# Four MLPs of a two-block transformer: the first product as seven block products in groups of four tiles, the second product behind each group

## The chip, the cores and the metric

The kernel runs on one core of one Trainium2 chip. The metric is device time in microseconds (us), the median of several executions; lower is better. The chip offers TensorE (matrix products, weight loads beside them), VectorE (DVE), ScalarE (ACT), GpSimd (POOL) and SyncE (SP), each working through its own queue in order, and DMA queues that bring weights from HBM.

## The reference

Two blocks of two layers each, in 32-bit floats. The stream is 512 tokens x 1024 features; the first layer of the first block also carries 256 context tokens through its MLP. Every layer ends in an MLP with squared ReLU, and these four MLPs are what the change is about:

```python
def _sq_relu_mlp(h, w1, w2):          # w1: 1024 x 4096, w2: 4096 x 1024
    a = jnp.maximum(h @ w1, 0)
    return (a * a) @ w2
# block 1, layer l:  x = _layer_norm(ALPHA * x + g2 * mlp(h), ...)   (l = 0: also for the 256 context tokens)
# block 2, layer i:  h_lat = h_lat + mod_l[5] * mlp(_modulate(_rmsnorm(h_lat, ...), ...))
```

The vectors g2, mod_l and their like come from matrix-vector products of a condition with a 1024 x 6144 matrix per layer.

## The kernel before

**Layout and precision.** Activations lie feature-major: 128 features on the partitions, tokens along the free axis (768 in the MLP `l0`, 512 in `l1`, `s0` and `s1`). A weight tile is 128 x 1024 floats, eight 128x128 blocks, 512 KB. Every product is made of three matmuls in a reduced format: both operands are split into a high part, rounded (`act_split`, ACT, L593, for weights), and a low part, the rest (`dve_split`, DVE, L624), and TensorE adds high x high, low x high and high x low. So each weight tile costs one ACT and one DVE instruction on 128x1024 and 24 matmuls per 512 tokens. `whi` has three slots for high parts (`NS`), so ACT can split tile i+2 once TensorE is through with tile i-1. Raw tiles land in four slots (`NR`), from the MLP `s0` on in nine (`XR` = 5 more; one more high slot, `XS`).

**Queues.** `Tiles` lists all weight tiles in the order in which TensorE uses them; `act_tiles` and `dve_tiles` bring the splits of the tiles ahead into ACT's and DVE's queues. All queues are written out at build time and strictly in that order; the engines meet at semaphores (`wait_ge`). A PSUM bank is claimed by TensorE for a result and freed by whoever read it (`claim`, `freed`).

**MLPs `l0`, `l1`** (`mlp`, `pe_mlp`, `act_mlp`, `dve_mlp`). Four rounds q; each makes eight fc1 tiles (ACT: ReLU out of PSUM L1253, DVE: square L1277, ACT: high part L1255, DVE: low part L1280), and then eight fc2 tiles over these eight, each added to the stream by DVE (`dve_add_gated`, L925: one instruction per 512 or 256 tokens). 

**MLPs `s0`, `s1`** (`second_mlp`, `pe_quads`, `act_quads`, `dve_quads`). The first eight fc1 tiles as above. The other 24 come in groups of four (Q = 2 to 7), each as seven block products after Strassen and Winograd: inputs and weights are cut in halves of features and tokens, four sums or differences of the input (`operand`, L2630 and L2636, once per MLP) and of the weights (`dve_block_sum`, L603, per group) are formed, and seven products replace eight (`product`, L2511: 24 matmuls of 256 tokens each). DVE adds the products out of PSUM into four cells of SBUF (`second_sums` L2658, L2663; `third_sums` L2671, L2675; `corner_sum` L2683), one for each quarter ("corner") of the result; ACT squares each (`corner_high`: ReLU L2582, high part L2584, square L2585), and DVE takes the low part (`corner_low`, L2688). After two groups come eight fc2 tiles. The last corner depends on the last product.

**Modulation jobs** (`modulation`, only in `l0`: 132 items, 128 of them tiles; and `s0`: 49, 48 tiles). They compute the condition vectors of later layers beside the MLP: for each tile ACT issues a 512 KB load (L692) into one of `NM` = 3 slots and DVE multiplies it with the condition and sums (L732). The items are dealt out evenly over steps 2 to 61 of the MLP's 64; a step stands at the same place of all queues:

```python
elif i in number:                     # ACT, in act_step, for the n-th tile of the step
    ACTQ.wait_ge(*at("dve_job", (name, n)))
    act_send(n + NM)
...                                   # DVE, in dve_step
    DVEQ.wait_ge(*at(f"job_in{n % NM}", (name, n)))
    dve.scalar_tensor_tensor(x, x, 1.0, sil[:, :], ...)
```

In `l0` a step follows each fc1 and each fc2 tile. In `s0` a step follows each of the first 16 tiles, and from then on two steps follow each fc2 tile and none stands among the block products (`second_steps`, L2485).

Of the kernel before, what the change touches and what calls it, by code (L numbers as in the profile page):

```python
# [13 lines left out]
P = 128  # L14
# [138 lines left out]
class Tiles:  # L153
# [46 lines left out]
    def place_blocks(self):  # L200

        first = min(self.start)
        G = self.alloc.index(self.keys[first])
        self.grown_at, self.slot, self.slot_after = first, {}, {}
        for a, key in enumerate(self.alloc):
            if G <= a < G + XR:
                self.slot[key], self.slot_after[key] = NR + a - G, ("mixout", 0)
# [4 lines left out]
        self.high, self.high_after = {}, {}  # L212
        for i, key in enumerate(self.keys):
            if first <= i < first + XS:
                self.high[key], self.high_after[key] = NS + i - first, ("mixout", 0)
                continue
            r = i - NS - (XS if i >= first else 0)
            before = self.keys[r] if r >= 0 else None
            self.high[key], self.high_after[key] = (i if before is None else self.high[before]), before

    def highs_upto(self, i):
        return min(i + NS + (XS if i >= self.grown_at - NS else 0) - self.hold[self.keys[i]], len(self.keys))

    def lows_upto(self, i):
        return min(i + NS - self.hold[self.keys[i]], len(self.keys))
# [49 lines left out]
XR, XS = 5, 1  # L275


class Parts:


    def __init__(self, parts):
        self.parts = parts

    def __getitem__(self, place):
        p, k, n = place
        return self.parts[k // 4][p, k % 4, n]


def quad_order(t, name):
    t.tile((name + "fc1", 0))  # L290
    t.tile((name + "fc1", 1), 1)
    for m in range(NK):
        if m > 1:
            t.tile((name + "fc1", m))
        t.mark((name, "evict", 0, m))
    for q in range(4):
        if q:
            t.quad(name + "fc1", 2 * q)
            t.quad(name + "fc1", 2 * q + 1)
        for m in range(NK):  # L300
            t.tile((name + "fc2", 8 * q + m))
    t.mark((name, "end"))


def mlp_order(t, name):
    t.tile((name + "fc1", 0))
    t.tile((name + "fc1", 1), 1)
    for q in range(4):
        for m in range(NK):
# [3 lines left out]
        for m in range(NK):  # L313
            t.tile((name + "fc2", 8 * q + m))
    t.mark((name, "end"))
# [64 lines left out]
def tile_order():  # L380
# [27 lines left out]
    quad_order(t, "s0")  # L408
# [3 lines left out]
    quad_order(t, "s1")  # L412
# [4 lines left out]
def program(nc, din, out, known):  # L417
# [77 lines left out]
    def high_of(key):  # L495
        n = seq.high[key]
        return whi[:, n, :] if n < NS else more["hi"][:, n - NS, :]
# [89 lines left out]
    def act_split(a):  # L587
# [3 lines left out]
        if seq.high_after[key]:  # L591
            ACTQ.wait_ge(*at("pe_tile", seq.index[seq.high_after[key]]))
# [34 lines left out]
    def act_tiles(upto):  # L627
        for key in seq.until("act", upto):
# [10 lines left out]
            for a in range(seq.come.get("hi", 0), seq.highs_upto(i)):  # L639
# [212 lines left out]
    def pe_dense(keys, Hh, Hl, hi_at, lo_at, ranges, bank=None, order=range(NK)):  # L852
# [8 lines left out]
        for k in order:  # L861
            PEQ.wait_ge(*hi_at(k))
            ws = slice(P * k, P * k + P)
            for key, acc, i, hi, lo in both:
                for w in (hi, lo):
                    for o, m, _ in ranges:
                        pe.matmul(acc.ap[:, o:o + m], w[:, ws], Hh[:, k, o:o + m], start=k == order[0] and w is hi, stop=False)  # L867
            PEQ.wait_ge(*lo_at(k))
            for key, acc, i, hi, lo in both:
                for o, m, _ in ranges:  # L870
                    ins = pe.matmul(acc.ap[:, o:o + m], hi[:, ws], Hl[:, k, o:o + m], start=False, stop=k == order[-1])  # L871
                if k == order[-1]:
# [280 lines left out]
    def ln_h(N, Hh, Hl):  # L1153
# [3 lines left out]
        act_ln_h(N, Hh)  # L1157
# [39 lines left out]
    def mlp(L, name, htag, ranges, Hh, Hl, after, centered, columns=None, beside=None, weights=None, jobs=None):  # L1197
# [4 lines left out]
        keys = [fc2(name, 3, m) for m in range(NK)]  # L1202
        with ExitStack() as s:
            Ah, Al = sb(s, [P, NK, n], F32R), sb(s, [P, NK, n], F32R)
            r1 = [sb(s, [P, n]) for _ in range(2)]
            r2 = [sb(s, [P, n]) for _ in range(2)]
            N = Norm(after, ranges, [sb(s, [P, n]) for _ in range(4)], centered, updated_at(keys, after, centered), weights)
            pe_by, act_by, dve_by = beside(s) if beside else [lambda t: None] * 3
            pe_step = act_step = dve_step = pool_all = None
            if jobs:  # L1210
                pe_step, act_step, dve_step, pool_all = modulation(name, sb(s, [P, 1024]), jobs, 2, 62)
            begin_stage("pool")
            pe_mlp(name, htag, ranges, Hh, Hl, Ah, Al, N, keys, pe_by, pe_step)
            act_mlp(L, name, n, Ah, r1, r2, N, act_by, act_step)
            if jobs:
                pool_all()
            dve_mlp(L, name, htag, ranges, n, Ah, Al, r1, r2, N, columns, dve_by, dve_step)
        return N

    def fc1(name, q, m):  # L1220
        return name + "fc1", 8 * q + m

    def fc2(name, q, m):
        return name + "fc2", 8 * q + m

    def pe_mlp(name, htag, ranges, Hh, Hl, Ah, Al, N, keys, beside, step):
        hh, hl = h_parts(htag)
        pe_dense([fc1(name, 0, 0), fc1(name, 0, 1)], Hh, Hl, hh, hl, ranges)
        for q in range(4):
            for m in range(NK):  # L1230
                if 8 * q + m > 1:
                    pe_dense([fc1(name, q, m)], Hh, Hl, hh, hl, ranges)
# [2752 lines left out]
```

## Time and profile before

| | |
|---|---|
| median of 3 runs | 3005.75 us (3005.33 to 3008.53) |
| the profiled execution | 3008.25 us, its span 3006.9 us |
| TensorE busy | 2856.6 us of the span, 16898 matmuls |
| DVE, ACT, POOL busy | 1736.5, 1146.9, 339.4 us |
| TensorE clock granted, mean | 0.981 of 2.4 GHz |
| MLP `l0`, from its first matmul to its last tile | 515.2 to 1065 us |
| MLP `l1` | 1452.7 to 1831 us |
| MLP `s0` | 2233.7 to 2590 us |
| MLP `s1` | 2640.6 to 2992 us |

A time of an instruction is from its start to its end as the profiler has it. Matmuls are pipelined, so the time that one costs in a stream is the length of a stretch over their number and not the duration shown. The same holds in small for DVE and ACT: of two instructions that follow each other, the second starts some 0.09 us before the first is shown to end.

### The profile page before, as it was taken

What the parts mean: (1) busy time and instruction counts of PE and PEld (TensorE: products, weight loads), DVE (VectorE), ACT (ScalarE), POOL (GpSimd) and SP (SyncE); (2) the same over time, 40 slices, a digit from 0 to 9 for tenths busy, and PEclk for the clock granted to TensorE, in tenths of its full rate; (3) what the DMA queues carried; (4) which work ended last, traced back from release to release, by engine and by line L of the source; (5) the groups of instructions that cost most, each with busy time, mean ns of one, the idle gap of its engine ahead of it and who ended that gap; (6) DMA issues with size and microseconds to landing.
All of it is one profiled execution on the core that took longest, in us unless ns stands there. A gap on an engine that the chain in (4) does not pass through costs nothing.

```text
span 3006.9 us, 41839 instructions
## 1 busy us (share of the span) xinstructions
PE 2856.6 (95%) x16898; PEld 2283.9 (76%) x16898; DVE 1736.5 (58%) x2638; ACT 1146.9 (38%) x1895; POOL 339.4 (11%) x371
## 2 busy tenths in 40 slices
PE   7999999999999989999999998998889999899998
PEld 6766667888888866767677776776667999679986
DVE  3656544656565656654554445646736888556664
ACT  4245443412222242554422334312643444444442
POOL 2022210300000030321201002000510000110000
PEclk9999999999999999999999999999999999999999
DMA  7222001556555511001232332312034555323321
GB/s 281 77 98 80 9 21 43 177 195 210 172 207 185 186 55 49 9 15 42 76 113 91 98 99 64 102 56 70 1 116 137 175 176 176 126 70 99 94 90 63
DMA packets 88487, 315.87 MB, mean 105 GB/s; under 512 B 9991, under 2 KB 12295, under 8 KB 88040
## 3 DMA queue, kind: packets, MB, share of 16 engines
q1 hardware_dynamic: 59040, 213.94, 21.8%
q10 hardware_dynamic: 29256, 99.26, 9.6%
q8 instruction: 135, 2.21, 0.3%
q14 instruction: 56, 0.46, 0.0%
HBM read 311.06 MB, written 2.10 MB: 104 GB/s over the span
## 4 chain that ended last, share of the span: by engine, by line
PE 55%; DVE 4%; ACT 3%; issue 1%; POOL 1%; ACTq 0%; DVEq 0%; POOLq 0%
PE bank L867 22%; PE bank L871 11%; PE bank L2511 8%; PE bank L1370 2%; PE bank L3484 2%; PE bank L1431 1%; PE bank L1387 1%; PE bank L1862 1%; PE bank L2257 1%; PE bank L1981 1%; PE bank L3256 1%; PE bank L977 1%; ACT t L593 0%; PE bank L3562 0%; PE bank L1379 0%
## 5 line engine op out<-in xcount | busy, mean ns | idle before, releaser
L867 PE MATMUL bank<-t 128*128 128x512 f32 x5600 | 1493.7, 369 | 28.5 <-ACT t L1173 7.5
L867 PEld LDWEIGHTS bank<-t 128*128 128x128 f32 x5600 | 958.7, 189 | 244.2 <-issue 51.8
L871 PE MATMUL bank<-t 128*128 128x512 f32 x2800 | 908.9, 368 | 5.9 <-POOL t L1182 5.7
L593 ACT ACTIVATE t<-t 128x1024 fp32r<-128x1024 f32 x386 | 404.9, 1054 | 708.6 <-PE bank L871 450.5
L624 DVE TENSOR_TENSOR t<-t 128x1024 fp32r<-128x1024 f32 x386 | 474.6, 1234 | 242.7 <-ACT t L593 240.9
L871 PEld LDWEIGHTS bank<-t 128*128 128x128 f32 x2800 | 478.3, 189 | 109.3 <-POOL t L1182 13.0
L925 DVE SCALAR_TENSOR_TENSOR t<-bank,t 128x512 f32<-128x512 f32 x192 | 129.6, 693 | 342.5 <-PE bank L871 327.4
L2511 PEld LDWEIGHTS bank<-t 128*128 128x128 f32 x2016 | 240.1, 189 | 0.5
L2511 PE MATMUL bank<-t 128*128 128x256 f32 x2016 | 240.2, 281 | 0.0
L732 DVE SCALAR_TENSOR_TENSOR t<-t 128x1024 f32<-128x1024 f32 x176 | 209.5, 1223 | 6.5 <-DMA t<-in_mod 6.2
L1571 POOL TENSOR_SCALAR t<-t 128x768 f32<-128x768 f32 (+3 forms) x160 | 126.2, 792 | 522.2 <-DVE t L1539 522.1
L1370 PE MATMUL bank<-t 64*128 64x384 f32 (+2 forms) x768 | 136.1, 472 | 16.5 <-ACT t L1469 5.2
L1514 DVE TENSOR_REDUCE t<-bank 128x1 f32<-128x768 f32 (+1 forms) x120 | 96.6, 845 | 88.2 <-PE bank L1379 68.0
L1459 ACT ACTIVATE t<-bank 128x384 f32<-128x384 f32 (+1 forms) x160 | 73.7, 460 | 171.9 <-PE bank L1387 171.5
L993 ACT ACTIVATE t<-t 128x512 f32<-128x512 f32 (+1 forms) x64 | 43.8, 685 | 248.1 <-DVE t L925 176.1
L1387 PEld LDWEIGHTS bank<-t 128*128 128x128 f32 x784 | 85.8, 141 | 59.2 <-issue 29.7
L1387 PE MATMUL bank<-t 128*128 128x128 f32 x784 | 121.2, 282 | 10.0 <-DVE t L1525 7.0
L1469 ACT ACTIVATE t<-bank,t 128x768 f32<-128x768 f32 (+3 forms) x160 | 124.3, 781 | 14.0 <-DVE t L1514 8.0
L1277 DVE TENSOR_TENSOR t<-t 128x768 f32<-128x768 f32 (+1 forms) x64 | 54.1, 845 | 94.1 <-ACT t L1253 94.1
L1431 PE MATMUL bank<-t 128*64 128x128 f32 x1568 | 105.1, 281 | 2.0 <-DVE t L1545 2.0
L1370 PEld LDWEIGHTS bank<-t 64*128 64x128 f32 x768 | 67.0, 188 | 52.3 <-issue 22.6
L1431 PEld LDWEIGHTS bank<-t 128*64 128x64 f32 x1568 | 85.7, 139 | 15.6 <-issue 13.2
(340 smaller groups left out, 2637.1 us busy)
## 6 DMA issues: line engine op xcount, KB each, us to landing
t<-in_mod ACTq DMA_DIRECT2D x176, 512.0 KB, 4.1
t<-in_l0fc SPq DMA_DIRECT2D x64, 512.0 KB, 3.9
t<-in_l1fc SPq DMA_DIRECT2D x64, 512.0 KB, 3.5
t<-in_s0fc SPq DMA_DIRECT2D x64, 512.0 KB, 3.6
t<-in_s1fc SPq DMA_DIRECT2D x64, 512.0 KB, 3.5
t<-in_mod SPq DMA_DIRECT2D x48, 512.0 KB, 4.4
t<-in_mixin SPq DMA_DIRECT2D x24, 512.0 KB, 3.4
t<-in_l0in SPq DMA_DIRECT2D x12, 512.0 KB, 3.6
```

Source lines behind the costliest of these rows:

```text
L593: act.activation(high_of(key), landed_of(key), ACT.Copy).then_inc(*up("act_whi", a))
L624: dve.tensor_tensor(low_of(key), landed_of(key), high_of(key).bitcast(F32), ALU.subtract).then_inc(*up("dve_wlo", a))
L732: dve.scalar_tensor_tensor(x, x, 1.0, sil[:, :], ALU.mult, ALU.mult, accum_out=modt[L][:, j, s:s + 1]).then_inc(*up("dve_job", (name, n)))
L867: pe.matmul(acc.ap[:, o:o + m], w[:, ws], Hh[:, k, o:o + m], start=k == order[0] and w is hi, stop=False)
L871: ins = pe.matmul(acc.ap[:, o:o + m], hi[:, ws], Hl[:, k, o:o + m], start=False, stop=k == order[-1])
L925: ins = dve.scalar_tensor_tensor(x[:, o:o + n], acc.ap[:, o:o + n], mcol(L, part, k, s), x[:, o:o + n], ALU.mult, ALU.add)
L1370: ins = pe.matmul(places[side][:, 512 * r + o:512 * r + o + m], g["q"][side](c), g["k"][side][:, k0:k0 + m], start=r not in begun, stop=last)
L1387: ins = pe.transpose(turns[r].ap[:, P * b:P * b + P], p[:, P * i:P * i + P], mat("ident"))
L1431: ins = pe.matmul(b6.ap[64 * side:64 * side + 64, 0:P], g["v"][side](kb), PT[(2 * u + side) % 3][:, r, b, :], start=i == 0, stop=i == len( ...
L1469: act.activation(keys_of(p, g), scores_of(ps[side], g), ACT.Exp, bias=row[:, 7:8], accum_out=row[:, 3:4]).then_inc(*ps[side].freed((tag, u ...
L1571: pool.tensor_scalar(x, x, stat(u, side)[:, 7:8], 1.0, ALU.mult, ALU.mult).then_inc(*up("pool_prob", (tag, u, side)))
L2511: ins = pe.matmul(bank.ap[:, 256 * pair:256 * pair + 256], w[:, ws], x, start=pair == 0 and k == 0 and w is hi and x is h, stop=pair == 1 ...
```

## The change

All four MLPs run one new routine `mlp`. Its group Q = 0 is four plain fc1 tiles; the groups Q = 1 to 7 are seven block products each. Behind each group stand four fc2 tiles of a new cut: each holds two output tiles (of eight) over the group's four fc1 tiles, so that every output is added to the stream eight times instead of four. In `l0` a product has 24 matmuls of 384 tokens and spans two PSUM banks (a pair called ps); there are three pairs, and the outputs use ps1 and ps0 in turn. The four operands are now formed before the four evictions of Q = 0, and their splits stand beside the first fc2 tiles. There are eight raw weight slots from `l0` on, and three high slots throughout. The input's plain copy (`F`) has eight buffers. The steps of the modulation jobs stand behind products 1, 3 and 5 and behind the fc2 tiles, two of them behind the second. A barrier between normalization and MLP in `l0` and `l1` falls away.

```diff
 BLOCKS = (0, 4, 5, 3)
 NR, NS, NM, NE = 4, 3, 3, 14
-XR, XS = 5, 1
+XR = 4
...
 def mlp_order(t, name):
     t.tile((name + "fc1", 0))
     t.tile((name + "fc1", 1), 1)
-    for q in range(4):
-        for m in range(NK):
-            if 8 * q + m > 1:
-                t.tile((name + "fc1", 8 * q + m))
-            t.mark((name, "evict", q, m))
-        for m in range(NK):
-            t.tile((name + "fc2", 8 * q + m))
+    for m in range(2, 4):
+        t.tile((name + "fc1", m))
+    for Q in range(8):
+        if Q:
+            t.quad(name + "fc1", Q)
+        for j in range(4):
+            t.tile((name + "fc2", 4 * Q + j))
     t.mark((name, "end"))
...
+    BLOCK_SUMS = {4: (1, 4, 5, ALU.add), 3: (4, 0, 4, ALU.subtract), 2: (2, 1, 0, ALU.subtract), 1: (6, 3, 2, ALU.subtract)}
...
     def dve_tiles(upto):
...
-                for a in range(seq.come.get("lo", 0), seq.lows_upto(i)):
+                dve_quad_sums(i, 2)
+                for a in range(seq.come.get("lo", 0), min(i + NS - seq.hold[key], len(seq.keys))):
                     dve_split(a)
-                dve_quad_sums(i)
+                dve_quad_sums(i, 4, 3, 1)
...
+    PRODUCT_BANKS = {NT: (0, 1, 2, 3, 0, 2, 3), T: (2, 0, 1, 2, 1, 2, 0)}
+    OUT_BANKS = {NT: (1, 0, 2, 3), T: (1, 0)}
...
+    def steps_beside(Q, p):
+
+        return (8 * Q + (p - 1) // 2,) if p in (1, 3, 5) else ()
+
+    def steps_behind(Q, j):
+
+        return ([8 * Q + 3], [8 * Q + 4, 8 * Q + 5], [8 * Q + 6], [8 * Q + 7])[j] if Q else (4 + j,)
...
+        def outputs(Q, j):
...
+            if j == 0:
+                for s in range(2):
+                    PEQ.wait_ge(*banks[s].claim(out_of(name, Q, 2 * j + s)))
+                for ks in ((1, 3), (0, 2)) if Q else ((0, 1), (2, 3)):
+                    for s in range(2):
+                        for k in ks:
+                            high(s, k, k == ks[0] and ks[0] < 2 and ks[0] == (1 if Q else 0))
+                    for s in range(2):
+                        for k in ks:
+                            low(s, k, k == ks[1] and ks[1] == (2 if Q else 3))
+                return
+            for s in range(2):
+                PEQ.wait_ge(*banks[s].claim(out_of(name, Q, 2 * j + s)))
+                for k in range(4):
+                    high(s, k, k == 0)
+                    low(s, k, k == 3)
...
+        for Q in range(8):
...
+            else:
+                for p in range(7):
+                    if p == 3:
+                        second_sums(Q)
+                    if p == 4:
+                        corner_sum(Q, 0)
+                    if p == 5:
+                        third_sums(Q)
+                    if p == 6:
+                        corner_sum(Q, 2)
+                    dve_tiles(quad(name, Q, p))
+                    if p in (5, 6):
+                        corner_low(Q, {5: 0, 6: 3}[p])
+                    if step:
+                        for s in steps_beside(Q, p):
+                            step(s)
+            for j in range(4):
+                if j == 0 and Q:
+                    corner_sum(Q, 1)
+                    corner_low(Q, 2)
+                    corner_low(Q, 1)
+                dve_tiles(fc2(name, Q, j))
...
+                if step:
+                    for s in steps_behind(Q, j):
+                        step(s)
+                for m in (2 * j, 2 * j + 1):
+                    update(Q, m)
```

`act_mlp` has the same shape: behind product p it runs `act_tiles`, at p = 4, 5 and 6 `corner_high` of corners 0, 3 and 2, then the steps; before the first fc2 tile `corner_high` of corner 1. `update` does what `dve_add_gated` did. The corners 0, 1, 2 and 3 rest on products 3, 6, 5 and 4.

## Rows read from the trace of the kernel before

**Rows 1.** The page's first part: busy us (share) x instructions; and the granted clock.

```profile
PE 2856.6 (95%) x16898; PEld 2283.9 (76%) x16898; DVE 1736.5 (58%) x2638; ACT 1146.9 (38%) x1895; POOL 339.4 (11%) x371
...
PEclk9999999999999999999999999999999999999999
```

**Rows 2.** Windows in `l0` and `s0`: length, busy us (x) by engine, clock, DMA.

```profile
721.80:789.00 67.20, 67.20 (x389) 58.66 (x388) 42.53 (x63) 11.19 (x13) 0.99 (x5) 1.00 0.62 210
2334.04:2374.05 40.01, 40.01 (x337) 40.01 (x337) 33.56 (x38) 27.00 (x37) 0.00 (x0) 1.00 0.46 149
2374.05:2418.63 44.58, 44.58 (x194) 36.04 (x194) 35.63 (x48) 10.49 (x12) 0.00 (x0) 1.00 0.62 196
```

**Rows 3.** Groups of PE by form: busy us, mean ns, idle before.

```profile
L2511 PE MATMUL bank<-t 128*128 128x256 f32 x2016 | 240.2, 281 | 0.0
...
L3484 PE MATMUL bank<-t 128*128 128x512 f32 x192 | 46.4, 398 | 1.9 <-DVE t L1746 1.7 <-DVE t L925 0.3
```

**Rows 4.** Line L2257 over the whole span: duration min/median/max of its two forms.

```profile
L2257 PE MATMUL bank<-t x240: 277/337/446, 164.6 to 1363.6; 128*128 128x384 f32 x72, 128*128 128x256 f32 x48
```

**Rows 5.** Groups of DVE in `l0`, 560 to 1000 us.

```profile
L732 DVE SCALAR_TENSOR_TENSOR t<-t 128x1024 f32<-128x1024 f32 x111 | 131.0, 1220 | 0.1
L624 DVE TENSOR_TENSOR t<-t 128x1024 fp32r<-128x1024 f32 x52 | 63.7, 1225 | 47.4 <-ACT t L593 46.4
L1280 DVE TENSOR_TENSOR t<-t 128x768 fp32r<-128x768 f32 x28 | 26.8, 958 | 25.5 <-ACT t L1255 25.5
...
L925 DVE SCALAR_TENSOR_TENSOR t<-bank,t 128x512 f32<-128x512 f32 x24 | 18.0, 750 | 65.4 <-PE bank L871 63.7 <-ACT t L722 1.6
L925 DVE SCALAR_TENSOR_TENSOR t<-bank,t 128x256 f32<-128x256 f32 x24 | 11.4, 475 | 0.0
```

**Rows 6.** Groups of ACT in `l0`, 560 to 1000 us.

```profile
L593 ACT ACTIVATE t<-t 128x1024 fp32r<-128x1024 f32 x53 | 56.2, 1061 | 264.4 <-PE bank L871 143.1 <-DVE t L732 121.3
L1255 ACT ACTIVATE t<-t 128x768 fp32r<-128x768 f32 x28 | 23.7, 846 | 31.5 <-DVE t L1277 31.5
```

**Rows 7.** Timeline of ACT in `l0`: start, us, instruction, idle before.

```profile
720.43 0.34 ACTq L692 DMA_DIRECT2D t<-in_mod  x1
720.81 1.06 ACT L593 ACTIVATE t<-t 128x1024 fp32r<-128x1024 f32 x1 [3.70 <-DVE t L732]
```

**Rows 8.** Timeline of DVE in `l0`, the same place.

```profile
719.17 1.22 DVE L732 SCALAR_TENSOR_TENSOR t<-t 128x1024 f32<-128x1024 f32 x1
...
721.98 1.23 DVE L624 TENSOR_TENSOR t<-t 128x1024 fp32r<-128x1024 f32 x1 [1.57 <-ACT t L593]
```

**Rows 9.** DMA issues of the page: KB each, median us from issue to landing.

```profile
t<-in_mod ACTq DMA_DIRECT2D x176, 512.0 KB, 4.1
```

**Rows 10.** Timeline of DVE in `s0`, from the fifth product's end on (group 3).

```profile
2368.46 0.69 DVE L2671 TENSOR_TENSOR t<-bank,t 128x512 f32<-128x512 f32 x1 [1.13 <-PE bank L2511]
...
2371.52 0.68 DVE L2683 TENSOR_TENSOR t<-bank,t 128x512 f32<-128x512 f32 x1
2372.13 1.21 DVE L624 TENSOR_TENSOR t<-t 128x1024 fp32r<-128x1024 f32 x1
...
2374.09 0.69 DVE L2683 TENSOR_TENSOR t<-bank,t 128x512 f32<-128x512 f32 x1
```

**Rows 11.** Timeline of ACT in `s0`, the same stretch.

```profile
2371.63 1.04 ACT L593 ACTIVATE t<-t 128x1024 fp32r<-128x1024 f32 x1
2372.58 0.62 ACT L2582 ACTIVATE t<-t 128x512 f32<-128x512 f32 x1
2373.22 0.63 ACT L2584 ACTIVATE t<-t 128x512 fp32r<-128x512 f32 x1
```

**Rows 12.** Timeline of PE: the stalls in the opening of `s0` and `s1`.

```profile
2256.49 0.70 PE L867 MATMUL bank<-t 128*128 128x512 f32 x2 [2.45 <-DVE t L624]
...
2292.07 0.73 PE L867 MATMUL bank<-t 128*128 128x512 f32 x2 [2.43 <-ACT t L2570]
...
2662.35 1.19 PE L867 MATMUL bank<-t 128*128 128x512 f32 x2 [2.58 <-DVE t L624]
```

**Rows 13.** Window of the opening of `s0`, columns as in Rows 2.

```profile
2290.00:2334.00 44.00, 41.93 (x173) 33.40 (x174) 30.41 (x37) 9.95 (x10) 0.00 (x0) 0.96 0.46 149
```

**Rows 14.** Groups of DVE in `l1`: the sine argument of the filter beside the MLP.

```profile
L2893 DVE SCALAR_TENSOR_TENSOR t<-t 64x512 f32<-64x512 f32 x6 | 4.1, 682 | 0.2
```

More of the change, by code:

```diff
@@ L495, in high_of @@
     def high_of(key):
-        n = seq.high[key]
-        return whi[:, n, :] if n < NS else more["hi"][:, n - NS, :]
+        return whi[:, seq.index[key] % NS, :]
     def landed_at(key):
@@ L638, in act_tiles @@
             i = seq.index[key]
-            for a in range(seq.come.get("hi", 0), seq.highs_upto(i)):
+            for a in range(seq.come.get("hi", 0), min(i + NS - seq.hold[key], len(seq.keys))):
                 act_split(a)
@@ L850, in program, with pe_dense @@
     acc_of = {}
-    def pe_dense(keys, Hh, Hl, hi_at, lo_at, ranges, bank=None, order=range(NK)):
+    def pe_dense(keys, Hh, Hl, hi_at, lo_at, ranges, bank=None):
         both = []
@@ L860, in pe_dense @@
             PEQ.wait_ge(*acc.claim(key))
-        for k in order:
+        for k in range(NK):
             PEQ.wait_ge(*hi_at(k))
@@ L866, in pe_dense @@
                     for o, m, _ in ranges:
-                        pe.matmul(acc.ap[:, o:o + m], w[:, ws], Hh[:, k, o:o + m], start=k == order[0] and w is hi, stop=False)
+                        pe.matmul(acc.ap[:, o:o + m], w[:, ws], Hh[:, k, o:o + m], start=k == 0 and w is hi, stop=False)
             PEQ.wait_ge(*lo_at(k))
@@ L1215, in mlp @@
             if jobs:
                 pool_all()
[L1217 to L1226, printed above, removed]
-        hh, hl = h_parts(htag)
[L1228 to L1232, printed above, removed]
-                if step:
-                    step(16 * q + m)
-            for m in range(NK):
-                pe_dense([fc2(name, q, m)], Ah, Al, lambda k: at("act_ahi", (name, q, k)),
-                         lambda k: at("dve_alo", (name, q, k)), ranges)
-                if q == 3:
-                    pe_norm_step(N, m, acc_of[keys[0]].after(keys[0]))
-                beside(8 * q + m)
-                if step:
-                    step(16 * q + 8 + m)
-        pe_tiles((name, "end"))
@@ L2741, in dve_quads, with second_mlp @@
-        dve_tiles((name, "end"))
+            dve.tensor_tensor(work[:, k % 4, :], XT[k][:, 0:NT], ps[2].ap[:, 0:NT], ALU.mult).then_inc(*done)
+        for k in range(NK):
+            POOLQ.wait_ge(*at("act_hhi", (N.tag, k)))
+            POOLQ.wait_ge(*at("act_h", (N.tag, k)))
+            pool.tensor_tensor(Hl[:, k, :], F[:, k, :], Hh[:, k, :].bitcast(F32),
+                               ALU.subtract).then_inc(*up("pool_hlo", (N.tag, k)))
+    def second_mlp(L, N, after, columns, jobs=None):
+        return mlp(L, f"s{L - 2}", N, LAT, after, False, lambda Hh, Hl, F, cells: second_h(N, L, Hh, Hl, F, cells),
+                   columns, jobs=jobs)
@@ L3552, in products @@
             PEQ.wait_ge(*ps[g % 2].claim(("pool v", g)))
-            for bank in fours[2 * (g % 2):2 * (g % 2) + 2]:
-                PEQ.wait_ge(*bank.after(bank.order[-1]))
             for kk in range(2):
```

753 lines of the change are left out of this document (331 added, 422 removed).

## The prediction

> **What bounds the kernel now.** I read the page first: TensorE is busy 95% of the span at a full clock [rows 1]. Then windows inside the MLPs, each cut from tile to tile: there TensorE never idles. Eight fc1 tiles of `l0` fill 67.2 of 67.2 us, two groups of block products in `s0` 40.0, eight fc2 tiles 44.6 [rows 2]. DVE stands at 63% in `l0` and at 80 to 84% in `s0`, ACT at 17 to 67%. Last the idle time of these two: DVE waits for ACT's splits, ACT for TensorE and for DVE's jobs [rows 5, 6]. So TensorE's stream sets the end, and DVE is the engine that comes next.
>
> **What the stream gains.** Per matmul: 44.58/192 = 0.232 us at 512 tokens, 40.01/336 = 0.119 at 256, and 67.2/192 = 0.350 for the pair 512 + 256 of `l0` [rows 2]. The trace has no long stream of 384. Durations shown are 281, 337 and 398 ns at 256, 384 and 512 [rows 3, 4], evenly spaced, so 384 lies midway between 0.119 and 0.232: 0.176. A plain group of four tiles has 96 matmuls per token range: 33.6 us in `l0`, 22.3 elsewhere. Seven products have 168: 29.6 and 19.95. Gain 4.03 us per group in `l0`, 2.33 elsewhere. Seven groups are new in `l0` (-28.2), seven in `l1` (-16.3), one each in `s0` and `s1` (-2.4 each): -49.3 us in all. fc2 has the same matmuls in another order, and the weight loads stay 64 tiles per MLP.
>
> For 384 columns the Trainium skill, "TensorE: Matmul & The Clock Gate", Back-to-back issue gap, gives N/2.4 + 2.5 ns. That is an estimate of 162.5 ns, and 28.2 would become 44. The rows are above that formula at both neighbouring widths (119 against 109, 232 against 216).
>
> **What DVE and ACT get.** A DVE instruction that follows another costs its duration less 0.09: 1.135 for a split or block sum, 0.87 for 768 tokens, 1.145 for a job, 1.06 for an update of 768 in two pieces [rows 5]. ACT: 0.95 a split, 0.75 for 768 [rows 6], 0.34 to issue a load [rows 7]. For one group of `l0` DVE does 11 splits (12.5), 4 block sums (4.5), 7 sums out of PSUM and 4 low parts (9.6), 8 updates (8.5, twice as many as now per group) and 17.6 jobs (20.2): 55 us in a TensorE group of 29.6 + 33.6 = 63.2. That is 87%, and behind the products 33 of 33.6. The queues are strictly in order, so what counts is what stands ahead of the instruction that TensorE waits for.
>
> **A group of `l0`, step by step.** I laid the three queues side by side in their new order; every instruction starts when the one ahead is through and what it waits for is there, 0.04 to 0.13 us after it. Group 3 stands for the rest (0 = start of product 0, products end every 4.22). Product 2 ends at 12.7. DVE: two sums, a split and the two jobs of the step at p = 3, until 18.1. ACT's split of the next tile stands behind its two sends, and each waits for its job. So it is now too: the split starts only after a job ends, and DVE's follows 1.57 us late [rows 7, 8]. Corner 0 until 19.0, split 20.8, third sums 21.2 to 23.0, split and low part to 25.1, three jobs of p = 5 to 28.5, corner 2 to 29.4, split (after ACT's) 31.2, low part 32.1. Only then comes corner 1, whose sum frees ps0, and ps0 is claimed by the first outputs: it ends 33.1, while TensorE was through at 29.6. **Stall 3.6.** With DVE on time it would still be 1.2, for the sum itself.
> From there (0 = first output, corner 1 freed) the first output is made at 7.7 and DVE, after two low parts, split, block sum and two jobs, updates it at 8.1 to 9.2; TensorE wants the bank back at 8.4. **Stall 0.8** (0.7 with no jobs). Then update, split, block sum, and two steps with four or five jobs. There are three load slots: the fourth job's load is sent after the first job and lands 4.1 us later [rows 9], so DVE waits 2.2 us and updates output 2 at 19.2 to 20.3; TensorE wants it at 17.6. **Stall 2.7 to 3.9.** The other outputs come in time. The same walk over all eight groups gives for Q = 1 to 7, 20.5 at the claim, 7.9 at output 2 and 25.7 at output 4; 3.7 more at Q = 7, where output 3 waits for the shift of the norm in the same bank; and 9.7 in Q = 0, where four operands of 1.7 us, their low parts and the updates crowd DVE. Together 67 us. `l0`: -28.2 + 67.4 = **+39**.
>
> **`s0`.** Four single banks take away the bank waits. But jobs now stand among the products, and TensorE's first output matmul needs corner 2. In the trace its sum runs at 2371.52, ACT's split at 2371.63, ReLU at 2372.58 and the high part 2373.22 to 2373.85; TensorE starts on fc2 at 2373.95 [rows 10, 11]: 0.1 us in hand. One job at p = 5 puts DVE's 1.145 and ACT's send (0.34) and wait ahead of that: high part at 2375.4, stall 1.4. A job at p = 3 too makes it 3.1, at all three 4.1. With 49 items over 60 steps the walk gives 17.6 for seven groups; 0.5 for low parts; 2.6 in Q = 0. Gone are the two stalls of the opening (4.9) [rows 12] and a half-rate stretch behind the second (44 us at a clock of 0.96 [rows 13], so 44 x 0.04 = 1.8 of lost cycles). `s0`: -2.4 + 20.7 - 6.7 = **+11.6**.
> **`l1`** has no jobs; each later group is just in time [rows 10, 11]. In Q = 0 DVE has splits, block sums, operand low parts, updates and the filter's sine arguments (two times 4.9, three instructions of 0.68 in each [rows 14]): 29 us in 22.3, which I price at 7.7 of stalls before product 2 of Q = 1; 1.1 of present ones go. -16.3 + 6.6 = **-9.7**.
> **`s1`** has neither: -2.4, and its stall of 2.6 [rows 12] with some 1.4 of half rate goes, 1.2 comes in Q = 0: **-5.2**.
> **Clock.** Behind two of the three stalls of 2.4 to 2.6 us the clock fell to half [rows 12, 13]; the cost was some 1.7 us each. `l0` and `s0` will have some 17 of that size. Part of it lies under DVE's lateness, so I take +5 (bounds 0 and 29).
> Weight slots, eight instead of four between the MLPs: no stall of TensorE outside them is put down to a load, so 0 (bounds -3, +1).
> Sum: 39.2 + 11.6 - 9.7 - 5.2 + 5 = 40.9 on a span of 3006.9. The profiled execution took 3008.25 against a median of 3005.75, 2.5 us that I do not carry over: 3005.75 + 40.9 = 3046.6, rounded to **3046**.
>
> The price of the queue order rests on strict order: DVE was idle for 1.57 us behind a job that ACT had to answer [rows 8]. The Trainium skill says the same of ACT and DVE, strict FIFO, in "TensorE: Matmul & The Clock Gate", Architectural detail; by it no later instruction slips past a job, and by the trace none does.
>
> **Rivals.**
> *The stalls of `l0` and `s0` are mostly absorbed* (other side). DVE's load is below 100% in every phase; if its instructions reach TensorE in time but for the structural 1.2 + 0.7 per group of `l0` and 3.7 at its end, `l0` has 19 us (-9), `s0` 3 (-6), with -9.7 and -5.2: -30, 2976; with nothing stalling at all -60, 2946. It decides from where the stalls of `l0` and `s0` together fall below 47 of 88 us. For it: DVE has some slack now [rows 5]. Against: its slack is not at the place of the chain. 0.20.
> *Half of the stalls*: the third load slot or the last corner is in time more often than I walk it. Within 6 us of before: 0.04; between 3012 and 3030, 0.10.
> *My forecast*, 3030 to 3065: 0.52.
> *The stalls let the clock fall each time*, 17 x 1.7 = 29 instead of 5, or job loads take 4.5 us (+5): 3065 to 3085. 0.09.
> *384 columns stream at 0.1625 or less.* As a mechanism: at 256 the weight load fills all of its queue, 40.01 of 40.01 us, in the longer ones it does not [rows 2], so the overhead of 384 may be smaller than midway. 1176 x 0.0135 = 16 us less stream in `l0`, of which DVE's lateness at the claim takes half: 3038. That rule of the skill's page is the reason to count it. 0.05.
>
> **The numbers.** Slower by over 0.2% (6 us, about what a measurement of this kernel can tell): 0.10 + 0.52 + 0.09 + 0.05 = 0.76. Same 0.04, faster 0.20. The range must leave out no more than 0.2: below 2980 I see 0.13 (of the absorbed case those near nothing stalling), above 3075 0.05, so 2980 to 3075. The forecast's own range, from its bounds (clock 0 to 15, `l1` opening 2 to 9, load time 3.3 to 4.5 giving -4 to +5): 3030 to 3065.
>
> **What the profile after would show.** TensorE idle in `l0` by some 67 us, ended by DVE's update and PSUM-sum lines, at the first, third and fifth output of each group; matmuls of 384 in products of 4.22 us; DVE waiting for `in_mod` loads some 2 us per group; in `s0` idle before each group's first output, ended by ACT's square; `l1` and `s1` shorter by 10 and 5 us, group time 42.2. I am wrong if a group of `l0` takes under 67 us from product 0 to product 0, if 384 columns cost more than 0.19 or less than 0.165, or if the stalls lie at weight splits instead of banks.

## The result, and the profile after

The changed kernel takes **3087.4 us** (median of 4 runs, 3081.4 to 3087.9) against 3006.3 for the kernel before on the same chip: ratio 1.026, 95% interval 1.025 to 1.028. Forecast were 3046, range 2980 to 3075. The sign and the stalls of TensorE came as forecast; the clock that they cost did not. The change is +81 us where +41 was forecast, and the time lies above the range.

The page of the changed kernel, the lines that answer to [rows 1, 9]:

```profile
PE 2847.5 (92%) x17378; PEld 2328.5 (75%) x17378; DVE 2031.5 (66%) x2974; ACT 1254.3 (41%) x2031; POOL 346.3 (11%) x371
...
PEclk9999999999999989999999999999999999999999
...
t<-in_mod ACTq DMA_DIRECT2D x176, 512.0 KB, 4.5
```

TensorE is busy for 9 us less in a span that is 80 us longer. Busy time alone would hide half of the loss: a matmul at half rate counts as busy. The windows of the four MLPs without their norms show both. Before (`l0`, `l1`, `s0`, `s1`), columns as in [rows 2]:

```profile
512.00:1066.00 554.00, 550.60 (x3154) 475.28 (x3156) 346.43 (x488) 149.88 (x176) 32.68 (x26) 0.99 0.54 182
1462.00:1829.00 367.00, 366.24 (x1561) 285.18 (x1560) 169.84 (x215) 122.83 (x165) 31.89 (x19) 1.00 0.31 99
2249.00:2590.00 341.00, 336.12 (x1932) 291.12 (x1931) 260.21 (x322) 145.91 (x188) 1.69 (x3) 0.99 0.52 173
2654.00:2992.00 338.00, 335.42 (x1931) 291.35 (x1930) 203.27 (x224) 141.75 (x183) 0.00 (x0) 0.99 0.27 86
```

After (in `l0` from the end of the opening on):

```profile
558.00:1134.00 576.00, 513.86 (x2788) 465.08 (x2788) 430.14 (x585) 170.96 (x193) 2.61 (x10) 0.95 0.51 169
1527.00:1892.00 365.00, 360.26 (x2102) 305.67 (x2100) 279.49 (x333) 172.40 (x232) 41.07 (x22) 0.99 0.32 100
2303.00:2674.00 371.00, 349.74 (x2051) 304.32 (x2049) 296.24 (x368) 158.97 (x206) 7.92 (x9) 0.99 0.49 158
2729.00:3073.00 344.00, 343.17 (x2043) 300.03 (x2043) 240.62 (x269) 156.71 (x203) 7.32 (x6) 1.00 0.28 86
```

`l0` is the place: 62 us idle in 576, and the clock at 0.95, where 1.00 is 2.4 GHz and the half-rate stretches run at 1.2. Who ended the idle time of TensorE (total, times, longest), first in `l0`, then in `s0`:

```profile
PE bank L1296 <- DVE t L1508: 36.5, 19, 5.2
PE bank L1296 <- DVE t L1462: 22.8, 7, 4.0
PE bank L1296 <- ACT t L1372: 7.4, 1, 7.4
```

```profile
PE bank L1296 <- DVE t L582: 19.1, 7, 4.2
```

L1508 is the update of the residual, L1462 a sum out of PSUM (here that of corner 1, which frees `ps0`), L1372 ReLU of a plain tile. L1296 are the matmuls of an fc2 output on the high parts of the activations, L1302 those on the low parts. In group 2 of `l0` one sees the claim, output 2 and output 4:

```profile
699.71 4.24 PE L1274 MATMUL bank<-t 128*128 128x384 f32 x23
707.15 4.60 PE L1296 MATMUL bank<-t 128*128 128x512 f32 x16 [3.21 <-DVE t L1462]
...
718.03 0.94 PE L1296 MATMUL bank<-t 128*128 128x512 f32 x4 [0.63 <-DVE t L1508]
...
725.11 0.51 PE L1302 MATMUL bank<-t 128*128 128x512 f32 x2
...
730.69 1.62 PE L1296 MATMUL bank<-t 128*128 128x512 f32 x4 [4.01 <-DVE t L1508]
732.11 0.84 PE L1302 MATMUL bank<-t 128*128 128x512 f32 x2
```

Behind the last stall two matmuls of L1302 take 0.84 us, before it 0.51. What DVE did until then, five jobs of two steps and their loads:

```profile
721.12 1.21 DVE L691 SCALAR_TENSOR_TENSOR t<-t 128x1024 f32<-128x1024 f32 x1
...
726.05 1.23 DVE L691 SCALAR_TENSOR_TENSOR t<-t 128x1024 f32<-128x1024 f32 x1 [1.42 <-DMA t<-in_mod]
...
728.26 1.23 DVE L691 SCALAR_TENSOR_TENSOR t<-t 128x1024 f32<-128x1024 f32 x1 [0.97 <-DMA t<-in_mod]
729.41 0.08 DVE L691 DVE_READ_ACCUMULATOR t<-t 128x1 f32 x1
729.41 2.19 DVE L1508 SCALAR_TENSOR_TENSOR t<-bank,t 128x512 f32<-128x512 f32 x4
```

And the clock around it, three windows (length, PE busy ..., clock):

```profile
657.04:660.45 3.41, 3.41 (x13) 2.93 (x12) 3.31 (x5) 0.00 (x0) 0.00 (x0) 0.50 0.06 25
728.72:735.55 6.83, 4.86 (x15) 4.21 (x16) 6.73 (x11) 1.06 (x1) 0.00 (x0) 0.50 0.48 153
783.33:790.15 6.82, 5.64 (x17) 4.84 (x18) 5.10 (x6) 3.48 (x5) 0.00 (x0) 0.50 0.07 29
```

In `s0` the walk's place, one group: a job at 2370.02, then the sum for corner 2, ACT's send, split, ReLU, high part, and TensorE.

```profile
2370.02 1.22 DVE L691 SCALAR_TENSOR_TENSOR t<-t 128x1024 f32<-128x1024 f32 x1
...
2371.16 0.68 DVE L1462 TENSOR_TENSOR t<-bank,t 128x512 f32<-128x512 f32 x1
```

```profile
2371.27 0.33 ACTq L651 DMA_DIRECT2D t<-in_mod  x1
2371.71 1.06 ACT L550 ACTIVATE t<-t 128x1024 fp32r<-128x1024 f32 x1 [1.76 <-DVE t L691]
2372.67 0.61 ACT L1389 ACTIVATE t<-t 128x512 f32<-128x512 f32 x1
2373.32 0.63 ACT L1391 ACTIVATE t<-t 128x512 fp32r<-128x512 f32 x1
```

```profile
2374.09 1.62 PE L1296 MATMUL bank<-t 128*128 128x512 f32 x3 [4.15 <-DVE t L582]
```

The trace puts this wait down to a weight split of DVE (L582), which ended at the same moment; the high part (L1391) ended at 2373.95, 0.14 before TensorE. The offsets are the same two in all seven groups, so this trace alone does not decide between them; both stand behind the job. In the sixth run, where the sum for this corner is what is late, the same wait is put down to the high part. It is the chain of [rows 10, 11], with a send and a wait for a job in it.

**Where the 80 us are.** I summed, over successive matmuls, the time from start to start less the spacing of that width (0.119, 0.176, 0.232): over 0.35 us it is a stall, inside a half-rate stretch it is clock. A stall costs 0.16 us more than its idle time, as the matmul ahead is shown until its pipelined end. The lengths are from one norm to the next. The rows add up to the 79.6 us between the two spans.

| us | forecast | measured | of it stalls | of it clock |
|---|---|---|---|---|
| `l0` | +39 | +71.7 | 0.9 to 72.6 | 1.3 to 23.7 |
| `l1` | -9.7 | -8.6 | 1.1 to 4.2 | 0 to 1.8 |
| `s0` mixer | 0 | +5.2 | - | not separated |
| `s0` | +11.6 | +16.6 | 5.2 to 22.7 | 1.6 to 4.7 |
| pool, rest | 0 | -1.3 | | |
| `s1` | -5.2 | -4.0 | 2.7 to 0.9 | 1.4 to 0 |
| clock | +5 | in the rows above | | |

### The profile page after: what moved, and what is told of

It reads as the page before. It is cut to its first block, busy times and chain, and to the rows that moved or that the text cites. A ratio compares the mean times of both kernels' runs of the same rounds, so it can differ in the third digit from the quotient of the medians.

```text
span 3086.5 us, 43456 instructions
## 1 busy us (share of the span) xinstructions
PE 2847.5 (92%) x17378; PEld 2328.5 (75%) x17378; DVE 2031.5 (66%) x2974; ACT 1254.3 (41%) x2031; POOL 346.3 (11%) x371
## 4 chain that ended last, share of the span: by engine, by line
PE 37%; DVE 6%; ACT 4%; issue 2%; POOL 1%; ACTq 0%; DVEq 0%; POOLq 0%
PE bank L1296 11%; PE bank L1274 10%; PE bank L1302 6%; PE bank L826 2%; ACT t L550 2%; DVE t L582 1%; PE bank L3436 1%; PE bank L830 1%; PE bank L2113 1%; ACT t L2681 1%; DVE t L691 1%; PE bank L1621 1%; PE bank L3213 1%; PE bank L936 1%; PE bank L3512 0%
## 5 line engine op out<-in xcount | busy, mean ns | idle before, releaser
L550 ACT ACTIVATE t<-t 128x1024 fp32r<-128x1024 f32 x434 | 456.1, 1054 | 853.1 <-PE bank L1302 352.0
L1296 PE MATMUL bank<-t 128*128 128x512 f32 (+1 forms) x2560 | 700.1, 384 | 88.7 <-DVE t L1508 36.5
L582 DVE TENSOR_TENSOR t<-t 128x1024 fp32r<-128x1024 f32 x434 | 538.3, 1244 | 334.7 <-ACT t L550 330.3
L1274 PE MATMUL bank<-t 128*128 128x256 f32 (+1 forms) x4704 | 632.9, 295 | 3.5 <-issue 2.5
L1274 PEld LDWEIGHTS bank<-t 128*128 128x128 f32 x4704 | 630.0, 188 | 6.8 <-issue 5.0
L1296 PEld LDWEIGHTS bank<-t 128*128 128x128 f32 x2560 | 458.3, 195 | 203.3 <-issue 99.2
L826 PE MATMUL bank<-t 128*128 128x512 f32 (+1 forms) x1568 | 414.1, 374 | 21.9 <-ACT t L1132 7.7
L1302 PE MATMUL bank<-t 128*128 128x512 f32 (+1 forms) x1280 | 408.5, 376 | 0.0
L826 PEld LDWEIGHTS bank<-t 128*128 128x128 f32 x1568 | 270.9, 194 | 88.8 <-issue 37.7
L1508 DVE SCALAR_TENSOR_TENSOR t<-bank,t 128x512 f32<-128x512 f32 x320 | 210.8, 692 | 88.8 <-PE bank L1302 88.1
L1302 PEld LDWEIGHTS bank<-t 128*128 128x128 f32 x1280 | 225.8, 192 | 48.6 <-DVE t L1489 3.4
L830 PE MATMUL bank<-t 128*128 128x512 f32 (+1 forms) x784 | 246.3, 371 | 6.7 <-POOL t L1141 6.6
L1462 DVE TENSOR_TENSOR t<-bank,t 128x512 f32<-128x512 f32 (+1 forms) x196 | 148.0, 755 | 30.2 <-PE bank L1274 25.4
L830 PEld LDWEIGHTS bank<-t 128*128 128x128 f32 x784 | 134.0, 192 | 37.6 <-POOL t L1141 11.7
L560 DVE TENSOR_TENSOR t<-t 128x1024 f32<-128x1024 f32 x112 | 140.7, 1256 | 0.0
```

Of the source, the lines that this page charges most:

```text
L550: act.activation(high_of(key), landed_of(key), ACT.Copy).then_inc(*up("act_whi", a))
L560: dve.tensor_tensor(landed_of(k[p]), landed_of(k[a]), landed_of(k[b]), op).then_inc(*up("dve_sum", k[p]))
L582: dve.tensor_tensor(low_of(key), landed_of(key), high_of(key).bitcast(F32), ALU.subtract).then_inc(*up("dve_wlo", a))
L1274: ins = pe.matmul(dst, w[:, ws], x, start=(pair == 0 or n > NT) and k == 0 and w is hi and x is high, stop=pair == 1 and k == 3 and x is l ...
L1296: pe.matmul(banks[s].ap[:, o:o + m], w[:, ws], Ah[:, k, o:o + m], start=first and w is hi, stop=False)
L1302: ins = pe.matmul(banks[s].ap[:, o:o + m], hi[:, ws], Al[:, k, o:o + m], start=False, stop=last)
```

## The experiments

Theory A: the stalls come from the order of the queues (jobs ahead of an update or a corner) and from two output banks that come back after one output; the half-rate time follows the long stalls. Against it stand: the clock belongs to the new stream (B), and DVE has simply too much to do, so the waits move (C). Each run is compared with runs of the kernel before on the same chip, 3007 to 3009 us. Runs 5 to 10 ran on another chip than the changed kernel and runs 1 to 4, so differences of a few us between the two sets say nothing. The edits are shown shortened, those of runs 2, 3 and 5 partly in words. What a run says of stalls and clock is summed as in the table, from its profiled execution.

**1. Three output banks in `l0`.**

```
-    OUT_BANKS = {NT: (1, 0, 2, 3), T: (1, 0)}
+    OUT_BANKS = {NT: (1, 0, 2, 3), T: (1, 2, 0, 1, 2, 0, 1, 0)}
+    LAST_BANKS = (2, 1, 0, 1, 0, 1, 0, 1)      # T, Q == 7
```

> The changed kernel, but fc2 of l0 goes round three output banks instead of two (ps1, ps2, ps0, ps1, ps2, ps0, ps1, ps0; in the last group ps2, ps1, ps0, ps1, ...). Nothing else moves. Theory A (stalls come from the order of the queues and the reuse of two banks; the half-rate clock follows the long stalls): by the same walk the stalls of TensorE in l0 fall from 71 to about 41 us (none at the claim of ps0 in groups 1 to 7, 1.1 to 2.2 before the second pair of cells' high parts, 0.8 to 1.9 at the sixth output instead of 2.7 to 4 at the fifth, 3.7 and 6.9 left in the last group), and with the stalls over 2.6 us gone from the middle the matmuls at half rate cost some 7 us instead of 24: 3087 - 30 - 17 = 3040. Theory B (the half-rate time belongs to the new stream itself, not to its stalls): stalls fall as in A, the 24 us stay: 3057. Theory C (DVE's load is the bound, so the stalls only go elsewhere): 3075 or more.

3041.5 us, ratio 1.0115 [1.010, 1.013]. Stalls of `l0` 72.6 to 40.3, clock 23.7 to 8.3. No claim waits for the corner any more; ACT's high part of it does:

```profile
PE bank L1298 <- DVE t L1510: 20.4, 10, 4.4
PE bank L1298 <- ACT t L1393: 11.7, 7, 2.3
```

**2. The steps of `l0` elsewhere**, banks as they were.

```
-  steps at products 1, 3, 5; fc2 tiles 0, 1, 1, 2, 3
+  steps at products 0, 2, 4; fc2 tiles 0, 1, 2, 3, 3
```

> The changed kernel, but the eight steps of the modulation jobs in a group of l0 stand behind products 0, 2 and 4, behind the first three fc2 tiles one each, and two behind the fourth (now: products 1, 3 and 5, fc2 tiles one, two, one, one). Banks as in the changed kernel. Theory A: by the walk the stalls of l0 fall from 71 to about 37 us (1.2 to 1.6 at the claim, 0.7 to 2.0 at output 2, none at output 4, 3.7 in the last group; the 3.8 and 4.0 of the first group stay), and the half-rate cost from 24 to about 7: 3087 - 34 - 17 = 3036. Theory B: 3053. Theory C (DVE's load): over 3075, stalls at other places.

3040.9 us, 1.0112 [1.010, 1.013]. Stalls 42.3, clock 7.9. The claims fell from 22.8 to 9.9 us in sum; output 4 waits only in groups 0 and 7:

```profile
PE bank L1298 <- DVE t L1510: 18.9, 12, 4.5
PE bank L1298 <- DVE t L1464: 9.9, 7, 2.0
PE bank L1298 <- ACT t L1374: 7.3, 1, 7.3
```

**3. The steps of `s0` behind fc2.**

```
-  steps at products 1, 3, 5; fc2 tiles 0, 1, 1, 2, 3
+  steps at product 2; fc2 tiles 0, 0, 1, 1, 2, 2, 3
```

> The changed kernel, but in s0 seven of the eight steps of a group stand behind the fc2 tiles (one behind product 2, two behind each of the first, second and third tile, one behind the fourth); l0 as it is. Theory A: the stalls in front of the first output of the seven groups fall from 20 to about 2 us, their half-rate cost from 4.7 to about 1: 3087 - 18 - 3 = 3066. Theory B: 3069. Theory C (the jobs' 1.145 us each come back as stalls at the outputs, whose four banks are then in use): 3080 or more.

3061.7 us, 1.0178 [1.016, 1.019], 4 us below theory A's 3066. `s0` is 358.8 us long instead of 382.7 (before the change 366.2), with 1.4 us of stalls. The 7.4 us below before fit the 2.4 of the products and the 4.9 of the two opening stalls that are gone [rows 12]. So all but 1.4 us of the stalls of `s0` were the jobs in the chain of corner 2.

**4. All three edits.**

> The three edits together: three output banks in l0, the steps of l0 at products 0, 2, 4 and behind fc2, those of s0 behind fc2. Theory A: stalls of l0 about 17 us (6 to 8 in the first group, 5 in the last), half-rate cost there about 5, s0 as in the third run: 3087 - 54 - 19 - 21 = 2993, faster than before the change by 0.4%. Theory B: 3012 to 3016, slower than before. Theory C: over 3050.

2995.2 us, 0.9962 [0.995, 0.997]: faster than before the change. Stalls of `l0` 23.0, clock 7.5. DVE is busy for 462 of 560 us there, 83%, more than the 75% of the changed kernel with its 72.6 us of stalls: against theory C, its load is not the bound.

**5. The products of `l0` undone**: plain fc1 tiles in groups of four; all else of the change stays.

```
-            t.quad(name + "fc1", Q)
+            if name == "l0": four plain tiles 4 * Q + m, evicted like those of group 0
+            (a step behind each fc1 and each fc2 tile; no operands, no corners)
```

> The changed kernel with one part undone: in l0 the seven later groups of fc1 are four plain tiles each again (24 x 768 tokens, 33.6 us per group instead of 29.6), with their eviction as in the kernel before; fc2 behind every four tiles, eight slots, and s0, l1 and s1 stay as changed. A step of jobs behind every tile. Theory A (the products' block sums, PSUM sums and corners are what makes DVE late in l0): stalls of l0 fall from 72 to under 8 us, half-rate cost from 24 to about 2, the stream grows by 28: 3087 - 65 - 22 + 28 = 3028 if 7 are left, and 3012 if l0 is what it was before (562.6 us). I expect 3012 to 3018. Theory B (fc2 by four tiles, with twice as many updates and its banks coming back at 8.4 us, makes the stalls by itself): 3040 or more. The four MLPs other than l0 then leave +6 to +9 against the kernel before.

3083.4 us, 1.0254 [1.024, 1.027]: my expectation fell, theory B's 3040 or more came. Without a single product `l0` is 628.7 us long, with them 634.4. Of its stalls, 44.8 us in all, nine wait for an update, seven of these 3.9 to 5.0 us long at output 2, and the clock costs 20.3 us as well:

```profile
PE bank L1303 <- DVE t L1529: 37.8, 9, 5.0
```

```profile
637.94 1.23 DVE L585 TENSOR_TENSOR t<-t 128x1024 fp32r<-128x1024 f32 x1 [1.57 <-ACT t L553]
639.09 1.22 DVE L694 SCALAR_TENSOR_TENSOR t<-t 128x1024 f32<-128x1024 f32 x1
...
641.38 2.19 DVE L1529 SCALAR_TENSOR_TENSOR t<-bank,t 128x512 f32<-128x512 f32 x4
```

```profile
642.66 0.77 PE L1303 MATMUL bank<-t 128*128 128x512 f32 x1 [5.03 <-DVE t L1529]
```

DVE's load is 351 us in the 576 of the window here, 61%. It is the order: three jobs stand behind the last fc1 tile, then the split that ACT's job send held up by 1.57 us, then two jobs, and then only the update that frees the bank. Before the change an output took 8.4 us and the bank was wanted 8.4 us later; by fours it is wanted after 4.2.

**6. Delays of known length in `s1`**, in the fourth run's kernel.

```
+            if name == "s1" and c == 2:        # ahead of the sum for corner 2
+                for _ in range(Q):
+                    dve.tensor_tensor(tabs[:, 3, :], tabs[:, 0, :], tabs[:, 1, :], ALU.add)
```

> The fourth run's kernel (all three edits) with a delay put in s1: ahead of the sum for corner 2 in group Q, DVE does Q extra additions of 128 x 512, one after the other, Q = 1 to 7. They are work left over, used by nobody. TensorE's first output waits for that corner, with some 0.1 us in hand, so its idle time should be about 0.7 Q: 0.6, 1.3, 2.0, 2.7, 3.4, 4.1, 4.8 us, sum 19. Theory A (the length of the idle time decides what the clock does): no half rate behind the first two or three, a half-rate stretch of 3.4 us behind the fourth and fifth, 6.8 us around the last two, in all some 9 us lost to half rate: 2995 + 19 + 9 = 3023. Theory B (each stall costs the same 1.7 us whatever its length): 7 stretches, 12 us, 3026, with stretches behind the short ones too. Theory C (it is the stream of 768 tokens in l0 that lets the clock fall, not idle time): none in s1, 3014.

3016.7 us in its single run. The seven idle times, group 1 to 7 (three are shown, 2.53, 3.26 and 3.99 lie between), and the clock behind those of groups 3 to 7:

```profile
2698.88 0.47 PE L1300 MATMUL bank<-t 128*128 128x512 f32 x1 [0.36 <-ACT t L1395]
...
2786.83 0.48 PE L1300 MATMUL bank<-t 128*128 128x512 f32 x1 [1.80 <-ACT t L1395]
...
2974.34 0.77 PE L1300 MATMUL bank<-t 128*128 128x512 f32 x1 [4.71 <-ACT t L1395]
```

```profile
2787.00:2831.00 44.00, 42.35 (x264) 37.88 (x263) 32.07 (x38) 17.83 (x23) 0.00 (x0) 1.00 0.32 96
2831.87:2877.00 45.13, 44.05 (x264) 39.14 (x264) 31.84 (x37) 17.56 (x22) 0.00 (x0) 0.96 0.31 94
2879.19:2924.00 44.81, 42.52 (x264) 38.00 (x264) 32.80 (x39) 17.55 (x22) 0.00 (x0) 1.00 0.31 95
2925.70:2970.00 44.30, 43.93 (x264) 39.11 (x264) 31.15 (x36) 17.56 (x22) 0.00 (x0) 0.96 0.19 60
2974.34:3000.00 25.66, 25.66 (x97) 18.89 (x98) 9.68 (x13) 7.94 (x13) 0.00 (x0) 0.89 0.00 1
```

Idle times of 0.4, 1.1 and 1.8 us have no half rate behind them, 2.53 has a stretch of 3.4 us, 3.26 none, 3.99 one of 3.4, 4.71 one of 6.8; 5.8 us are lost. So idle time makes the clock fall in `s1` too, whose products have 256 columns (against C), the cost grows with the length (against this run's B), and in the middle it is not decided by the length alone. The stalls came to 19.6 us, `s1` grew by 24.4 against the fourth run: a delay in this chain goes through in full.

**7. Narrow jobs**: a job's instruction reads 64 of 1024 columns.

```
-  dve.scalar_tensor_tensor(x, x, 1.0, sil[:, :], ...)
+  dve.scalar_tensor_tensor(x[:, 0:64], x[:, 0:64], 1.0, sil[:, 0:64], ...)
```

> The changed kernel, but a job's instruction on DVE reads 64 of its 1024 columns, so the modulation vectors made in l0 and s0 are sums over 64 columns instead of 1024; the loads, their three slots, the waits and the order stay. Theory A (it is the jobs' 1.145 us on DVE that stand ahead of what TensorE waits for): by the walk stalls of l0 fall from 71 to about 33 us (1.2 at each claim, 0.7 at output 2, 0.7 to 1.1 at output 4), those of s0 from 23 to 6, half-rate cost from 29 to about 9: 3087 - 38 - 17 - 20 = 3012. Theory B (it is the jobs' loads, three slots and 4.1 to 4.5 us each, so the stalls at output 4 stay): 25 us more, 3035 or over.

3010.8 us, 1.0011 [1.000, 1.002], for a kernel whose modulation vectors are sums over 64 columns, so it computes something else. Loads, slots and waits are unchanged, and 77 us are gone: it is the 1.145 us on DVE. Left in `l0` are the claims (9.4 us, seven), the first group (6.3) and 15.2 at updates.

**8. The fourth run, jobs of `l0` from step 4 on** (`modulation(..., 4, 62)`).

> The fourth run's kernel with the jobs of l0 spread over steps 4 to 62 instead of 2 to 62, so none of them and no copy of the condition stands between the first group's four plain tiles. By the walk the stalls of the first group fall from some 8 to 1 to 3 us and 1.1 us each come at two products later: 2995 - 3 to - 6 = 2989 to 2992. Theory C (the first group's stalls are those of DVE's operands and their low parts, not of the jobs): 2995, no change.

2992.1 us, 0.9951 [0.994, 0.997]. The stalls of the first group fell from 10.6 to 3.8 us; against the fourth run's 2995.2 the difference is no larger than the spread of either, so the size is inconclusive.

**9. Plain groups in `l0` with three output banks.**

> The fifth run's kernel (plain tiles in all groups of l0) with three output banks instead of two in groups 0 to 6. The fifth run had one stall of 3.9 to 5.0 us in each group, at output 2, for the update of output 0. Theory D (the stalls come from the bank's early return together with the jobs that stand ahead of the update; the products themselves are not needed for it): the third output takes a bank that is free, the update is wanted 4.2 us later, the seven stalls fall from 32 to under 5 us in sum (the last group's 3.9 stays twice, its banks are two), half-rate cost from 20 to about 6: 3083 - 27 - 14 = 3042. Theory E (DVE has too much to do in a group, so the wait moves to outputs 4 and 6): 3070 or more.

3040.6 us, 1.0105 [1.009, 1.012]. Stalls of `l0` 44.8 to 17.1, clock 20.3 to 5.7. In groups 1 to 6 at most one idle time of 0.2 to 0.8 us is left, and the last group's two of 3.9, whose banks are two:

```profile
638.47 0.49 PE L1305 MATMUL bank<-t 128*128 128x512 f32 x1 [0.75 <-DVE t L1531]
...
1046.18 0.76 PE L1305 MATMUL bank<-t 128*128 128x512 f32 x1 [3.90 <-DVE t L1531]
```

`l0` is 585.1 us long, with products and three banks (first run) 587.8, with 40.3 us of stalls and 8.3 of clock. So with the jobs where the change put them, the products' gain of 24 to 28 us is eaten by their own stalls. (The steps of the plain version stand behind every tile, so the two differ in that too.)

**10. A fourth bank in the last group**, on top of the eighth run.

```
-    LAST_BANKS = (2, 1, 0, 1, 0, 1, 0, 1)
+    LAST_BANKS = (2, 1, 0, 3, 1, 0, 3, 1)      # 3: b6 and b7 as one
```

> The eighth run's kernel, but in the last group of l0 the fc2 outputs 3 and 6 take the fourth pair of banks (b6 and b7 together), which the jobs no longer need there, so that they don't wait for the updates behind the shift of the norm. The eighth run had 3.9 us of stall at output 3 and 4.5 at output 4 there, and some 3 us of half rate. Theory A: both go, 2992 - 8 - 3 = 2981. Theory F (DVE stays late through the group, because each update there has the norm's subtraction ahead, and the time comes back at the sums of the norm): 2988 to 2992.

2983.7 us, 0.9920 [0.9905, 0.9934], the fastest version here. `l0` is 553.8 us long (before the change 562.6) with 11.5 us of stalls and 0.7 of clock. A part of theory F holds too: the norm behind the MLP now waits 4.4 us instead of 3.4.

## Why the prediction was right and wrong

**The stream**: right. 384 columns take 0.177 us on average, median 0.178, against my 0.176; a product of 24 takes 4.24. The Trainium skill, "TensorE: Matmul & The Clock Gate", Back-to-back issue gap, has N/2.4 + 2.5 ns as the gap of an isolated matmul at full clock, an estimate of 162.5 ns at 384; in this stream of weight load and matmul the trace does not agree, and the rival of 3038 fell. One small slip: by [rows 2] seven products of 256 take 20.0 us and not 19.95, 0.4 us less gain in all.

**The stalls**: right in place, in the chain that made them, and in size. Idle time of `l0` 66.7 us against 67.4: the claims 22.8 (20.5), output 2 6.4 (7.9), output 4 20.9 (25.7), output 3 of the last group 3.9 (3.7), group 0 11.6 (9.7), output 6 of the last group 1.0 (none). The terms are off by up to 4.8 us in both directions, so that the sums differ by 0.7 is in part luck. `s0` 21.1 against 20.7, the longest 4.15 against 4.1. A group of `l0` took over 70 us, and no stall lay at a product's split. The 0.16 us that each stall costs beyond its idle time, some 4 us in `l0`, were not in the walk.

**The clock**: the step that failed. "Part of it lies under DVE's lateness, so I take +5 (bounds 0 and 29)." In `l0` alone it cost 22 us more than before, in `s0` 3, where I had taken 1.8 off. With `l1` (+1.8) and `s1` (-1.4) that is 26 us; the sum has +5 - 1.8 - 1.4, about 2. These 24 us are the larger part of the 39 by which the sum missed the span.

The count and the price were not at fault: 17 stalls at 1.7 us, 29 us, against 28.4 in `l0` and `s0` (23.7 and 4.7). In part that is luck. `l0` and `s0` have 18 idle times of 2.5 us or more, and 14 have a half-rate stretch; eight are 3.4 us long and lost 1.2 to 1.6 us each, six are 6.8 us long and lost 1.9 to 2.7. Of the 13 idle times of 2.65 us or more in `l0`, 11 have one; of the 14 under 2 us none. What was wrong is the discount: the loss does not lie under DVE's lateness. The idle time came out as walked while the clock's loss came on top of it, and the runs that took the long stalls away (1, 2, 4, 7, 9) got 15 to 18 us of clock back besides. So the rival that I gave 0.09, "the stalls let the clock fall each time", had this step right. With its 29 in place of 5 the sum is 3070.6, still inside the range; the 0.16 us per stall, the mixer and some 6 us of `l0`, both told below, took the time above it. I had also named 29 as the bound of this term and then carried only 15 into the forecast's own range.

The Trainium skill, "TensorE: Matmul & The Clock Gate", Terms, prices a half-rate time at about itself x (1 - K/N). The MLP `l0` has 64 us at half, an estimate of 32; 23.7 is measured. 10 of the 64 us are idle time, and a matmul of 256 columns goes from 0.119 to 0.21 us at half rate, not to twice.

**The rest**: `l1` and `s1` came within 1.2 us of their terms, `l1` with 3.1 us more of stalls where I had walked 6.6. The stretch of `s0`'s mixer, which I held at 0, took 5.2 more. No edit touched it, and over all runs its length goes with its half-rate time: from the last sums of the norm behind `l1` to the norm ahead of `s0` it is 394.8 us with 20.5 at half before, 396 to 397 with 24 to 27 in runs 3, 4, 6 and 8, and 400 to 401 with 36 to 40 in the changed kernel and the other runs. That points to the clock for this term too; no run isolates it, and why the half-rate time differs from run to run is open. Some 6 us of `l0` belong to none of the columns of the table; 2.3 of them are the wait of the norm behind the MLP for ACT's squares (L928), 3.38 us against 1.11 before, and 1.6 are the 0.177 us per matmul of 384 against 0.176.

**What the prediction did not ask.** It blamed the products' DVE work for the lateness in `l0`. The fifth run has two thirds of the loss without products, 65 us of stalls and clock against 96: fc2 by four tiles with two banks, and jobs ahead of the update, are enough for that. The other 31 come with the products (and with the places of the steps, which the fifth run moved too), about what their shorter stream gains. The causes overlap: taking the products away gave 4 us, no more than the spread of the runs, while the banks (run 1), the steps of `l0` (run 2) and those of `s0` (run 3) gave 46, 46 and 26 one by one and 92 together.

## What to carry to other kernels

When a loop is cut in half, ask for every buffer by how much sooner it must come back, and keep side work (here the jobs) off the place ahead of the instruction that frees it; the load of that engine (75% in `l0`, 61% in the fifth run, 83% in the fourth) says little, the order of its queue decided. Price a stall of TensorE by its length and add the price in full: the idle time shown, 0.16 us on top, and the clock. Over the changed kernel and the ten runs, all 46 idle times of 3.5 us and more in the products and outputs had half rate at their end or just behind it, 20 of 39 between 2.4 and 3.4 us, 5 of 15 between 2 and 2.4, and 2 of 87 between 1 and 2 us. A stretch lost 1.2 to 2.7 us.

## What the runs showed of the hardware

- Half rate is no function of the idle time alone: 2.53 us had a stretch behind it and 3.26 us, 44 us later in the same stream, none; in `l0`, 2.73 had none and 2.69 one. One and the same stall of the first group of `l0` was followed by full clock in the fourth run (2.82 us, 1.00 over the next 9 us) and by a half-rate stretch in the sixth (2.81 us, 0.82), whose kernel differs in `s1` alone.
- A long stretch begins before the stall ends: that at 728.72 covers 2 us of idle time and ends 4.9 us after TensorE went on. A short one can begin behind it: that at 657.04 starts 1.4 us after TensorE went on at 655.58.
- Job loads landed in 4.5 us instead of 4.1 [rows 9] with the same bytes. With the jobs narrow and the loads as they are, at most 1.1 us are left at output 4 of groups 1 to 6, so this was not the price.
